# First mixer of the second block: six of eight output panels as three rounded products

## What is computed

```python
y = group_norm_heads(jnp.moveaxis(y, 0, 1), ln_g, ln_b, RW_LN_EPS)
bonus = jnp.sum(rh * kh * r_k, axis=-1, keepdims=True) * vh
y = (y + bonus.reshape(b_, s_, RW_WIDTH).astype(F32)) * g.astype(F32)
...
h = jnp.concatenate([y_a, y_b], axis=-1) @ ev_w_out[i]
...
x = x + rms_norm_2(h, ng[3])
```

## Time and profile before

| | us |
|---|---|
| median of 3 runs | 2246.55 (2245.90 to 2247.49) |
| profiled execution, its time | 2246.66 |
| its span, first to last instruction | 2244.8 |
| output panels of this stage | 1379.27 to 1406.91, 27.64 |

### The profile page before, as it was taken

The page is one execution under the profiler, slowest core; times in us unless marked ns, Lnnn a source line. Parts: engine busy times, 40 slices in busy tenths (PEclk is TensorE's granted clock), DMA queues, the critical chain, the costliest instruction groups (busy, mean ns, idle before and its releaser), DMA issues.

```text
span 2244.8 us, 39620 instructions
## 1 busy us (share of the span) xinstructions
PE 2157.0 (96%) x16004; PEld 1893.5 (84%) x16004; DVE 1492.6 (66%) x2407; ACT 929.6 (41%) x1448; POOL 43.6 (2%) x37
## 2 busy tenths in 40 slices
PE   6999999999999999999999999999999999899997
PEld 3655688888888599999998987789989999688997
DVE  4779664444455866676667785586686677656666
ACT  3225532222233844454444452454454453344444
POOL 0000000000003000000001100000000000000000
PEclk9999999999999999999999999999999999999999
DMA  7768323223223055556554311355646654143653
GB/s 290 272 247 299 113 80 104 94 94 103 94 86 103 1 170 196 192 170 200 193 192 150 125 56 58 103 173 193 194 153 197 194 172 142 56 141 123 196 196 123
DMA packets 93558, 338.91 MB, mean 151 GB/s; under 512 B 10224, under 2 KB 12400, under 8 KB 93168
## 3 DMA queue, kind: packets, MB, share of 16 engines
q1 hardware_dynamic: 92096, 331.84, 44.4%
q10 hardware_dynamic: 1328, 5.21, 0.6%
HBM read 335.96 MB, written 1.05 MB: 150 GB/s over the span
## 4 chain that ended last, share of the span: by engine, by line
PE 86%; DVE 7%; ACT 4%; DMA 2%; issue 1%; SPq 0%; DVEq 0%; ACTq 0%
PE ps L559 21%; PE ps L561 21%; PE ps L560 21%; PE ps L985 2%; PE ps L666 2%; DMA ring<-weights 2%; PE ps L1256 1%; DVE WS L2098 1%; PE ps L582 1%; ACT HS L1851 1%; PE ps L571 1%; PE ps L1067 1%; PE ps L932 1%; PE ps L1090 1%; ACT WS L1539 1%
## 5 line engine op out<-in xcount | busy, mean ns | idle before, releaser
L2098 DVE TENSOR_TENSOR WS<-ring,WS 128x1024 fp32r<-128x1024 f32 x484 | 593.1, 1229 | 338.0 <-ACT WS L1539 337.1
L559 PE MATMUL ps<-HS,WS 128*128 128x256 f32 x2928 | 809.8, 277 | 6.6 <-DVE WS L2098 4.5
L561 PE MATMUL ps<-HS,WS 128*128 128x256 f32 x2928 | 805.9, 275 | 0.0
L560 PE MATMUL ps<-HS,WS 128*128 128x256 f32 x2888 | 794.7, 275 | 0.0
L1539 ACT CAST WS<-ring 128x1024 fp32r<-128x1024 f32 x484 | 506.5, 1049 | 546.5 <-PE ps L561 450.9
L559 PEld LDWEIGHTS ps<-HS,WS 128*128 128x128 f32 x2928 | 549.7, 188 | 10.3 <-DVE WS L2098 4.5
L561 PEld LDWEIGHTS ps<-HS,WS 128*128 128x128 f32 x2928 | 549.7, 188 | 0.0
L560 PEld LDWEIGHTS ps<-HS,WS 128*128 128x128 f32 x2888 | 542.2, 188 | 1.0 <-issue 1.0
L559 PE MATMUL ps<-CH,WS 128*128 128x512 f32 (+1 forms) x464 | 176.5, 380 | 0.3 <-DVE WS L2098 0.3
L560 PE MATMUL ps<-CH,WS 128*128 128x512 f32 (+1 forms) x464 | 173.9, 375 | 0.0
L561 PE MATMUL ps<-CH,WS 128*128 128x512 f32 (+1 forms) x464 | 173.8, 375 | 0.0
(11 more groups left out here) (426 smaller groups left out, 2672.4 us busy)
## 6 DMA issues: line engine op xcount, KB each, us to landing
ring<-weights SPq DMA_DIRECT2D x630, 512.0 KB, 3.7
X<-xs ACTq DMA_DIRECT2D x1, 2048.0 KB, 8.7
con<-const ACTq DMA_DIRECT2D x1, 2016.0 KB, 9.7
X<-mem ACTq DMA_DIRECT2D x1, 1024.0 KB, 5.6
y<-X SPq DMA_DIRECT2D x4, 256.0 KB, 2.2
vecs<-vec SPq DMA_DIRECT2D x1, 311.5 KB, 7.3
con<-const SPq DMA_DIRECT2D x1, 130.0 KB, 8.5
```

What stands on the lines that cost most here:

```text
L559: pe.matmul(dst, w[0][:, cut], upper, start=first, stop=False, skip_group_check=True)
L560: pe.matmul(dst, w[0][:, cut], lower, start=False, stop=False, skip_group_check=True)
L561: return pe.matmul(dst, w[1][:, cut], upper, start=False, stop=last, skip_group_check=True)
L2098: dve.tensor_tensor(WS[:, split % HALVES, 1, :], ring[:, panel % RING, :], WS[:, split % HALVES, 0, :].bitcast(F32), ALU.subtract).then_in ...
```

## The change

- Rows 0 to 3 and 6 to 7 of the output product become rounded products (`split_rows_out`, two sections `m0_out` and `m0_last`); rows 4 and 5 (`y_a` tiles 0 and 1) stay plain.
- The operand for these rows is split: ScalarE writes `YU` for tiles 4 to 7 (`m0_out_high`) and 2 to 3 (`m0_last_high`), VectorE writes what is left into `LOWERED` (`row_lowers`).
- ScalarE adds the shift `rw_b` to `BON` ahead of time (four activations), and VectorE's gain and shift become one fused multiply-add with `BON`; the separate sum with `BON` goes, and each half of `Y` is gated as soon as it is ready (`ya1`, `ya3`).

```diff
+        LOWERED = {4: stored[:, 8220:8220 + 4 * T].rearrange("p (k t) -> p k t", k=4),
+                   2: stored[:, 9244:9244 + 2 * T].rearrange("p (k t) -> p k t", k=2)}
...
+            def split_rows_out(tag, section, first, last):
+
+                split_section(section, last - first)
+                y0 = (first + 4) % KT
+                pe.wait_ge(dve_done, at("dve", f"{section}_low"))
+                for r in range(first, last):
+                    w = split_panel()
+                    for k in range(KT):
+                        ins = three_products(ACC(k), w, slice(k * P, (k + 1) * P), YU[:, (r + 4) % KT, :],
+                                             LOWERED[y0][:, r - first, :], r == 0 and k % 2 == 0, r == KT - 1)
+                        if r == KT - 1 and k in (1, 3, 5):
+                            s.step(ins.then_inc(pe_done, 1), f"{tag}.acc{k // 2}")
+                    ins.then_inc(splits_used, 1)
+                    plan["split", f"{tag}_out{r}"] = splits[0]
...
-            row_products(*m0_out, 0, 4)
-            row_products(*m0_out, 4, 8)
+            split_rows_out("m0", "m0_out", 0, 4)
+            row_products(*m0_out, 4, 6)
+            split_rows_out("m0", "m0_last", 6, 8)
...
+            act.wait_ge(dve_done, at("dve", "rw_bonus"))
+            for m in range(4):
+                s.step(act.activation(BON[:, m, :], BON[:, m, :], ACT.Identity, bias=v("rw_b", m)).then_inc(act_done, 1), "rw_shifted")
+            uppers("m0_out", 0, 3)
+            act.wait_ge(dve_done, at("dve", "yb3"))
+            s.step(act.copy(YU[:, 4:KT, :], Y[:, 4:KT, :]).then_inc(act_done, 1), "m0_out_high")
             for t in range(2):
                 act.wait_ge(pe_done, at("pe", f"rw_y{t}"))
...
             act.activation(small[:, 1:2], eps6, ACT.Sqrt)
-            post_norm("m0", lambda b: ("pe", f"m0.acc{b}") if b < 3 else ("native", "m0_out7"))
+            upper("m0_out", 3)
+            uppers("m0_last", 0, 2)
+            act.wait_ge(dve_done, at("dve", "ya3"))
+            s.step(act.copy(YU[:, 2:4, :], Y[:, 2:4, :]).then_inc(act_done, 1), "m0_last_high")
+            post_norm("m0", lambda b: ("pe", f"m0.acc{b}") if b < 3 else ("split", "m0_out7"))
...
+            def row_lowers(section, first, count):
+
+                part = slice(first, first + count)
+                dve.wait_ge(act_done, at("act", section + "_high"))
+                s.step(dve.tensor_tensor(LOWERED[first], Y[:, part, :], YU[:, part, :].bitcast(F32),
+                                         ALU.subtract).then_inc(dve_done, 1), section + "_low")
```

More of the change, by code:

```diff
@@ L1379, in _ @@
             m0_rows = lambda r: (r + 4) % KT
-            m0_out = ("m0", KT, lambda r: Y[:, m0_rows(r), :], lambda r: ("dve", f"yb{r}" if r < 4 else f"ya{r - 4}"))
-            row_products(*m0_out, 0, 4)
-            row_products(*m0_out, 4, 8)
+            m0_out = ("m0", KT, lambda r: Y[:, m0_rows(r), :], lambda r: ("dve", "ya1"))
+            split_rows_out("m0", "m0_out", 0, 4)
+            row_products(*m0_out, 4, 6)
+            split_rows_out("m0", "m0_last", 6, 8)
             sums_post("m0")
@@ L2816, in _ @@
                     s.step(dve.tensor_tensor(SKP, SK[:, ch, :, :], PC[:, :, ch:ch + 1].to_broadcast([P, 4, 64]), ALU.mult).then_inc(dve_done, 1))
+                    if ch == 0:
+                        lowers("m0_out", 0, 2)
                     dve.wait_ge(pe_done, at("pe", f"rw_s{ch + 1}"))
@@ L2820, in _ @@
                                              SKP, ALU.add).then_inc(dve_done, 1), f"rw_s{ch + 1}")
+            row_lowers("m0_out", 4, 4)
             dve.wait_ge(pe_done, at("pe", "rw_y1"))
@@ L2823, in _ @@
             dve.wait_ge(dve_done, s.n)
+            lower("m0_out", 2)
             centered("rw", YR, 64, 0)
             for q in range(2):
[L2826 to L2832, removed]
+                pairs, gate = YR[:, 2 * q:2 * q + 2, :], RWG[:, 2 * q:2 * q + 2, :]
+                dve.wait_ge(act_done, at("act", f"rw_rms{q}"))
+                s.step(dve.reciprocal(WRR[:, q, :], WRR[:, q, :]).then_inc(dve_done, 1))
+                if q == 0:
+                    lower("m0_out", 3)
+                dve.wait_ge(dve_done, s.n)
+                s.step(dve.tensor_tensor(pairs, pairs, two(WRR[:, q, :]), ALU.mult).then_inc(dve_done, 1))
+                dve.wait_ge(dve_done, s.n)
+                dve.wait_ge(act_done, at("act", "rw_shifted"))
+                for m in (2 * q, 2 * q + 1):
+                    s.step(dve.scalar_tensor_tensor(out=YR[:, m, :], in0=YR[:, m, :], scalar=v("rw_g", m), in1=BON[:, m, :],
+                                                    op0=ALU.mult, op1=ALU.add).then_inc(dve_done, 1))
+                dve.wait_ge(dve_done, s.n)
+                s.step(dve.tensor_tensor(Y[:, 2 * q:2 * q + 2, :], pairs, gate, ALU.mult).then_inc(dve_done, 1), f"ya{2 * q + 1}")
+            lower("m0_last", 0)
+            row_lowers("m0_last", 2, 2)
+            lower("m0_last", 1)
             post_norm("m0", "x0")
```

## The result

The changed kernel takes 2252.07 us (median of 13 runs, 2250.66 to 2255.36), the kernel before beside it 2246.62 us (13 runs): a ratio of 1.0023, 95% interval 1.0016 to 1.0030, so 5.45 us slower by the medians. Forecast were 2247.5 us and "same". The profiled execution of the changed kernel took 2250.71 us, its span is 2248.8 us, 4.0 us more than before, and its mean granted clock 0.988, before 0.991.

What follows compares the result with a forecast made beforehand. TensorE's products were taken to bound the panels, a TensorE-VectorE chain the recurrence. Panels -3.75, switch +0.2, stall +3.4, `row_lowers` +0.1 and clock +1.0 gave +0.95 us on 2246.55: 2247.5 us, own bounds 2246.2 to 2248.7, 8-in-10 range 2244.8 to 2250.2.

Steps and rivals of the forecast that it cites:

- the one given 8%: Whole kernel: the change makes it slower, by more than about 0.2% (4.5 us); chance 0.08.
- What bounds the stage: Output panels bound by TensorE's own products; the recurrence before them by a chain of small steps between TensorE and VectorE.
- The panels: Output product: six panels as 24 rounded products, 0.118 us each, 2.83 us and not 3.455, save 3.75 us (4.35).
- the switch: Output panels, from plain to rounded products at row 6: costs 0.2 us, another 0.2 at most at row 0.
- The stall: Recurrence: two VectorE `lower` steps wait for ScalarE's cast and delay the first state's sum by 3.4 us (3.2 to 3.7).
- `row_lowers`, group norm, the shifts: `row_lowers` before the recurrence's last copy costs 0.1 us; group norm by halves lies beside TensorE and gives nothing.
- TensorE's clock: Recurrence behind the stall: TensorE's pause brings 1.2 GHz for a while, costing 1.0 us (0.5 to 1.7).
- my longest case: Low clock through the recurrence: 1.7 us, and 1.6 for one more group of 32 products and two of 16.
- The clock stays down until the panels: Rival: low clock from 1367 through group norm costs 6.0 us, time 2252.5 us; chance 0.09.
- The clock holds: Rival: same stall in the recurrence but no low clock, -0.05 us in all, 2246.5 us; chance 0.24.
- the stall is not there: Rival: the two `lower` steps fit VectorE's wait of 2.98 us, sum -3.45, 2243.1 us; chance 0.10.

Runs made afterwards that it cites:

- the first experiment: Changed kernel with the first two `lower` steps moved out of the recurrence, behind its last copy and the centring; 2242.62 us, ratio 0.9979 to the kernel before.
- second experiments: Changed kernel with seven unread products ahead of TensorE's wait for the first state; 2245.70 us, ratio 1.0000 to the kernel before.
- the pause alone: Kernel before, all panels plain, with six unread VectorE subtractions where the changed kernel has its `lower` steps; 2257.35 us, ratio 1.0046.
- the sixth experiment: Changed kernel with ScalarE's three casts ahead of its four shifts; 2248.81 us, ratio 1.0013 to the kernel before.
- the seventh: Changed kernel with three unread products in TensorE's pause; 2249.65 us, ratio 1.0015 to the kernel before.

## Why the prediction was wrong

The time (2252.07) lies 4.6 us above the forecast and above its range, and the direction was the one given 8%. In the profile's terms the clock cost 3.7 us more than its term, and the panels gave 0.7 us more than theirs, which hid a part of the miss. Point by point:

- **What bounds the stage: right.** Panels by TensorE alone, the recurrence by its chain; whatever is put into VectorE's queue and doesn't fit its waits delays the end.
- **The panels: right in kind, mis-sized.** Forecast 3.75 less 0.2 at the switch, 3.55; measured 4.27, a little beyond its other end too (4.35 less 0.2). The spacing is 0.118 us only for the first ten products or so of a section and 0.113 after, so four panels took 10.94 us and not 11.32; at the switch to row 6 the chain shows steps of 0.12 and no 0.2. In the kernel before, all 120 products of the second mixer's output stood 0.118 apart. I had put that down to operands in `HS2` and `HID`; these panels have the same and ran at 0.113, so it isn't that. The rule of the Trainium skill that true FP32 takes four passes ("FP8 and Floating Point Precision", section "TensorE Precision Notes") gives 5.2 us as an estimate; the trace still disagrees with it, by 0.9 us and not by 1.4.
- **The stall: right.** 3.4 forecast, 3.37 in the profile; the first and second experiments differ by 3.1 (medians) or 4.7 (ratios).
- **`row_lowers`, group norm, the shifts: right.** 0.10 and nothing.
- **TensorE's clock: this term failed.** I saw that the pause would bring 1.2 GHz, and took 1.0 us for it, with 1.7 as its upper bound. It cost 4.7 us in the profile. Two things went wrong. *How long*: I allowed one or two stretches as long as that of the earlier trace rows, because after 1325.6 the same small products had brought the clock back. In three kernels (the changed one in both its profiles, the pause alone, the casts first) it stayed low for some 13.6 us, four times as long, with TensorE busy, in the changed kernel, for 3.38 to 3.40 of 3.40 us with 53 to 60 records of products, no less than in the row (3.16 of 3.30, 60 records). One case was taken as a rule. *How much in that time*: my longest case put 1.7 + 1.6 = 3.3 us on the recurrence; it was 4.7. The three stages from sum to sum and to the copy lose 1.2, 2.3 and 1.2 us, where I had doubled two groups of x32 and four of x16 and no more (I called the records products; the sums don't change by it). In the chain of waits of the changed kernel, at half clock, TensorE waits for nobody from 1367.77 to 1382.02, and its unread product (L1379, two records), which filled a wait before, now stands on the path:

```profile
1373.44 0.85 PE ps L1342 x13
1374.29 1.15 PE ps L1379 x2
1375.44 1.79 PE ps L1357 x29
```

In the chain of the first experiment, with the clock at 1.00, VectorE's addition stands between the same two groups of products:

```profile
1368.93 0.47 PE ps L1342 x15
...
1369.77 0.42 DVE arena L2845
1370.23 1.08 PE ps L1357 x29
```

- **The rivals.** *The clock stays down until the panels* gave 2252.5, and the time came to that by luck: the 2.7 us of it behind the recurrence did not happen in the profile. The clock was back at 1380.4, and means and squares ran at full speed; the recurrence lost 4.7 us and not its 3.3. I gave it 9% on the single recovery at 1329. *The clock holds* and *the stall is not there* were neither; the first experiment shows what the second of these would have given, 2242.62 (2243.1 in the text, for the same sum without a stall).

The profile's terms sum to 3.9 us; the medians say 5.45 and, on another chip, 4.1. In the same way the clock is worth 4.7 to 5.2 us by the rows (4.72; second profile: 1370.78 to 1385.96 from sum to copy, 15.18 less 10.01) and 6.4 us by medians of different groups of runs (2252.07 less 2245.70; 2257.35 less 2250.96). By the ratios, each taken beside the kernel before, it is 5.2 and 6.3 us, and the whole change costs 5.2 and 4.7. So most of what the profile leaves open lies within the scatter of the runs; whether some of it is real stays open. Open too: why one stretch sufficed for the clock at 1329 and four were needed here, and what sets the spacing of the products, 0.118 or 0.113.

## What to carry over

When an edit makes one engine late in a tight chain of hand-overs, price the pause of TensorE twice: the stall itself, and everything on the path behind it at 1.2 GHz until the end of the chain of small products, not only as long as the clock was low at another place of the trace; an unread product that covered a wait at full clock belongs to that path. Put preparation work for a later stage where its inputs are already there (here behind the last copy of the recurrence), even if an earlier wait of the engine looks just large enough for it; its inputs' arrival and not its length decides. If such a pause can't be avoided, unread products in it keep the clock: seven of them gave back 5 to 6 us here.

## What the runs showed of the hardware

- A pause of 3.47 us between 64x64 products brought TensorE to 1.2 GHz in both profiles of the changed kernel, one of 1.89 us did in the sixth experiment, and one of 1.98 us did not in the seventh.
- The low clock lasted some 13.6 us in four profiles of three kernels, with TensorE busy by its records nearly throughout; it cost 4.7 to 5.2 us each time, more than the stall before it (3.2 to 3.4, in the sixth experiment 1.8).
- Where VectorE was as full (3.14 of 3.30 us), a low clock cost 0.65 us in the profile of the kernel before, though TensorE's own products were slower by more; filling the pause at 1324 removed the fall, and its worth is too small for the medians to tell (0.9996, interval 0.9987 to 1.0005).
- A panel as 24 rounded products took 2.74 to 2.76 us against 3.455 for eight plain products: 0.71 us saved by each of the six.
